# The residual as the first term of the experts' sums, and a final norm that reads PSUM

## What is computed

```
x = x + mixed @ w_merge_out
h = rms_norm(x, norm2_g)
logits = h @ router_w + router_b            # 32 experts, the top 4 of each token
f = sum over the top 4 of gate * (act @ w_down[e] + b_down[e])
    act = (up + 1) * (g * sigmoid(1.702 * g)),  [g, up] = h @ w_gate_up[e] + b_gate_up[e], clamped at 7
x = x + f
y = rms_norm(x, final_norm_g)
```

## Time and profile before

| | |
|---|---|
| median of 3 runs | 1508.98 us (1508.48 to 1509.87) |
| the profiled execution | 1509.2 us, its span 1507.0 us |
| mean granted clock of TensorE | 0.95 |
| PE busy | 1401.1 us, 93% |
| PEld busy | 655.4 us, 43% |
| DVE busy | 353.7 us, 23% |
| ACT busy | 178.6 us, 12% |
| HBM read | 440.53 MB |

### The profile page before, as it was taken

One profiled execution on the slowest core, in us unless ns is written; L12 is line 12 of the kernel. 1 busy time (PEld: TensorE's weight loads), 2 busy tenths in 40 slices (PEclk: granted clock), 3 DMA queues, 4 the chain that ended last, 5 costly groups with the idle time before them and its releaser, 6 DMA issues.

```text
span 1507.0 us, 15701 instructions
## 1 busy us (share of the span) xinstructions
PE 1401.1 (93%) x6182; PEld 655.4 (43%) x6183; DVE 353.7 (23%) x935; ACT 178.6 (12%) x348; POOL 36.6 (2%) x44
## 2 busy tenths in 40 slices
PE   6997998998989999999998999999999999999886
PEld 4775776896444333333332333333333333332222
DVE  2496626333551101111010101100110011001002
ACT  2011252210010100001000001000001000000002
POOL 3101001000000000000000000000000000000000
PEclk9999997987966999999999999999999999999998
DMA  9648212014455999999980999999999999999925
GB/s 251 139 139 88 84 56 57 1 57 141 170 217 204 416 416 418 417 417 414 418 358 2 414 415 416 418 416 416 416 418 417 415 415 417 418 415 415 414 105 214
DMA packets 86364, 446.52 MB, mean 296 GB/s; under 512 B 9456, under 2 KB 10368, under 8 KB 53360
## 3 DMA queue, kind: packets, MB, share of 16 engines
q1 hardware_dynamic: 82960, 436.45, 73.8%
q0 software_dynamic: 2720, 7.13, 1.9%
q10 hardware_dynamic: 576, 1.37, 0.3%
HBM read 440.53 MB, written 4.39 MB: 295 GB/s over the span
## 4 chain that ended last, share of the span: by engine, by line
PE 72%; DMA 21%; DVE 3%; issue 2%; SPq 1%; ACT 1%; ACTq 0%; DVEq 0%
PE ps L1048 21%; DMA arena<-in_w_gate_up 17%; PE ps L1076 10%; PE ps L711 10%; PE ps L1027 6%; PE ps L1086 3%; PE ps L929 2%; PE ps L1041 2%; DMA arena<-in_w_down 1%; DMA arena<-in_w_main 1%; SPq L359 1%; PE ps L922 1%; PE ps L816 1%; PE ps L750 1%; PE ps L1127 1%
## 5 line engine op out<-in xcount | busy, mean ns | idle before, releaser
L1048 PE MATMUL ps<-arena 128*64 128x512 f32 x2048 | 460.0, 602 | 13.1 <-DMA arena<-in_w_gate_up 12.9
L1048 PEld LDWEIGHTS ps<-arena 128*64 128x64 f32 x2048 | 145.6, 138 | 326.2 <-issue 277.9
L1076 PE MATMUL ps<-arena 128*64 128x512 f32 x1024 | 227.3, 595 | 10.1 <-issue 6.8
L1590 DVE TENSOR_SCALAR arena<-ps 128x512 f32<-128x512 f32 x32 | 22.1, 692 | 726.4 <-PE ps L1048 726.4
L711 PE MATMUL ps<-arena 128*128 128x320 f32 x576 | 161.8, 444 | 14.2 <-DMA arena<-in_w_main 8.5
L1076 PEld LDWEIGHTS ps<-arena 128*64 128x64 f32 x1024 | 82.8, 137 | 132.4 <-issue 127.1
L711 PEld LDWEIGHTS ps<-arena 128*128 128x128 f32 x576 | 112.4, 196 | 63.3 <-issue 19.3
L1027 PE MATMUL ps<-arena 128*128 128x256 f32 (+1 forms) x384 | 121.7, 447 | 0.0
L1027 PEld LDWEIGHTS ps<-arena 128*128 128x128 f32 (+1 forms) x384 | 67.8, 204 | 66.3 <-issue 61.9
L1086 PE MATMUL ps<-arena 128*128 128x512 f32 (+1 forms) x192 | 79.4, 617 | 1.3 <-ACT arena L619 1.3
L608 ACT ACTIVATE arena<-ps 128x512 f32<-128x512 f32 x32 | 19.1, 597 | 478.7 <-PE ps L1048 478.7
(11 more groups left out here) (288 smaller groups left out, 920.1 us busy)
## 6 DMA issues: line engine op xcount, KB each, us to landing
arena<-in_w_gate_up SPq DMA_DIRECT2D x256, 1024.0 KB, 20.2
arena<-in_w_down SPq DMA_DIRECT2D x128, 1024.0 KB, 23.8
arena<-in_w_main SPq DMA_DIRECT2D x40, 512.0 KB, 3.6
arena<-in_w_merge_out SPq DMA_DIRECT2D x1, 3072.0 KB, 10.5
arena<-in_w_conv_out POOLq DMA_DIRECT2D x1, 2048.0 KB, 13.1
arena<-in_w_delta_out SPq DMA_DIRECT2D x1, 2048.0 KB, 9.0
out_delta_s<-arena POOLq DMA_DIRECT2D x1, 2048.0 KB, 15.1
arena<-in_xT SPq DMA_DIRECT2D x1, 1280.0 KB, 6.6
```

The costliest lines, as they stand in the source:

```text
L1048: m = pe.matmul(ps[SLOTS * (q % 2):SLOTS * (q % 2 + 1), q // 2, :], tokens[:, k], w[:, q * 512:(q + 1) * 512], start=False, stop=(k == KD ...
L1076: m = pe.matmul(ps[SLOTS * c:SLOTS * (c + 1), 2, :], actT[:, r, a * SLOTS:(a + 1) * SLOTS], pieces[UPS + r][:, a, c * 512:(c + 1) * 512], ...
L1590: ts(upb, ps[:, 1, :], 1.0 + LIMIT, 1.0 - LIMIT, ALU.min, ALU.max).then_inc(chain, 1)
```

## The change

`bias` gets a matmul with the identity ahead of the one with the gates: `xs` of the tile is the moving operand, so the residual is the first term of the sum in the bank, and the biases are added to it. `add_sums` is gone. ScalarE squares the sums where they stand in PSUM as soon as the tile's last `combine` is through; for `t` 2, whose halves lie on different partitions, in two instructions with a second row sum (`stat_2`), which VectorE adds. `final_norm` scales from PSUM too. A new semaphore `rest_over` tells ScalarE that the code of `any_rest` is behind VectorE.

```
@@ -156,7 +156,7 @@
         con_at = at[0]
         ident = take(P)
         iota = take(PLACED)
-        stat, stat_y, stat_t = take(NT), take(NT), take(NT)
+        stat, stat_2, stat_y, stat_t = take(NT), take(1), take(NT), take(NT)
         late_at = at[0]
         h2 = take(2, D)
         actb = take(512)
@@ -189,6 +189,9 @@
         late_y, late_xt = upb[0:2 * LATE], sil[0:2 * LATE]
         late_actT = actT[:, :, 0:2 * LATE]
         assert moe[0] <= base
+        def sums(t):
+            return ps[:, 3 + 2 * t:5 + 2 * t, :].rearrange("p b n -> p (b n)")
+
         def rows(t):
 
 
@@ -671,9 +674,15 @@
 
             for t in range(NT):
                 n = TILES[t][1]
-                act.wait_ge(sem("added"), 2 * (t + 1))
-                act.activation(yout[0:n, t], xs[0:n, t], ACT.Square,
-                               accum_out=stat[0:n, t:t + 1]).then_inc(sem("x2_ss"), 1)
+                act.wait_ge(sem("rest_over"), 1)
+                act.wait_ge(sem("c_mm"), 2 * NT * (E // 2 - 1) + 2 * (t + 1))
+                if t < 2:
+                    act.activation(yout[0:n, t], sums(t), ACT.Square,
+                                   accum_out=stat[0:n, t:t + 1]).then_inc(sem("x2_ss"), 1)
+                else:
+                    act.activation(yout[0:n, t, 0:512], ps[0:NS, 7, :], ACT.Square, accum_out=stat[0:n, t:t + 1])
+                    act.activation(yout[0:n, t, 512:D], ps[NS:P, 7, :], ACT.Square,
+                                   accum_out=stat_2[0:n]).then_inc(sem("x2_ss"), 1)
                 root(stat_y[0:n, t:t + 1], stat[0:n, t:t + 1], 8 + t)
 
         @block.tensor
@@ -991,8 +1000,11 @@
                 return pe.transpose(ps[0:E, 0, tok(t)], gates[rows(t), t, 0:E], ident[rows(t), rows(t)])
 
             def bias(t, c, out):
+                n = TILES[t][1]
+                pe.matmul(out, ident[0:n, 0:n], xs[0:n, t, c * 512:(c + 1) * 512],
+                          start=True, stop=False, skip_group_check=True)
                 pe.matmul(out, gmT[0:E, tok(t)], bdn[0:E, c * 512:(c + 1) * 512],
-                          start=True, stop=True, skip_group_check=True).then_inc(sem("bd_mm"), 1)
+                          start=False, stop=True, skip_group_check=True).then_inc(sem("bd_mm"), 1)
 
             pe.wait_ge(sem("x2_done"), 6)
             pe.wait_ge(sem("gates_ready"), 2)
@@ -1628,6 +1640,7 @@
                     over(late_later[0:1].unsqueeze(1), 1, E, LATER), ALU.is_gt))
             link(dve.tensor_reduce(hot_most[0:1], ps[0:1, 1, NT * E:(NT + 1) * E], mybir.AxisListType.X, ALU.max))
             link(ts(hot_now[0:1], hot_most[0:1], float(REST), None, ALU.is_gt))
+            step.done(dve.memset(stat_2, 0.0))
             dve.memset(stat, 0.0).then_inc(sem("routed"), 1)
             ts(bg[2 * E:], bg[2 * E:], 1.0, None, ALU.add).then_inc(sem("bg_ready"), 1)
             for u in range(4):
@@ -1681,26 +1694,26 @@
             def final_norm(t):
                 n, col = TILES[t][1], slice(t, t + 1)
                 dve.wait_ge(sem("x2_ss"), NT + t + 1)
+                if t == 2:
+                    link(tt(stat[0:n, col], stat[0:n, col], stat_2[0:n], ALU.add))
                 ts(stat[0:n, col], stat[0:n, col], 1.0 / D, EPS, ALU.mult, ALU.add).then_inc(sem("root_in"), 1)
                 root(stat_y[0:n, col], stat[0:n, col], stat_t[0:n, col], 8 + t)
-                stt(out=yout[0:n, t], in0=xs[0:n, t], scalar=stat_y[0:n, col], in1=fg[0:n],
-                    op0=ALU.mult, op1=ALU.mult).then_inc(sem("y_out"), 1)
-
-            def add_sums(t):
-                n = TILES[t][1]
-                dve.wait_ge(sem("c_mm"), 2 * NT * (E // 2 - 1) + 2 * (t + 1))
-                for c in range(2):
-                    part = xs[0:n, t, c * 512:(c + 1) * 512]
-                    src = ps[:, SUM_BANKS[t][c], :] if t < 2 else ps[NS * c:NS * (c + 1), SUM_BANKS[t][c], :]
-                    tt(part, part, src, ALU.add).then_inc(sem("added"), 1)
-
-            add_sums(0)
-            add_sums(1)
+                if t < 2:
+                    stt(out=yout[0:n, t], in0=sums(t), scalar=stat_y[0:n, col], in1=fg,
+                        op0=ALU.mult, op1=ALU.mult).then_inc(sem("y_out"), 1)
+                else:
+                    for c in range(2):
+                        i = stt(out=yout[0:n, t, c * 512:(c + 1) * 512], in0=ps[NS * c:NS * (c + 1), 7, :],
+                                scalar=stat_y[0:n, col], in1=fg[0:n, c * 512:(c + 1) * 512],
+                                op0=ALU.mult, op1=ALU.mult)
+                        if c == 0:
+                            step.done(i)
+                    i.then_inc(sem("y_out"), 1)
+
+            dve.sem_inc(sem("rest_over"), 1)
             dve.wait_ge(sem("ld_fg"), 16)
-            final_norm(0)
-            add_sums(2)
-            final_norm(1)
-            final_norm(2)
+            for t in range(NT):
+                final_norm(t)
 
 
 INS = [("xT", (P, KD, N)), ("x_prompt", (NP, D)), ("x_sample", (NS, D)),
```

## The result

The changed kernel takes 1525.24 us (median of 4 runs, 1517.56 to 1528.66); the kernel before, run beside it, 1508.73 us (4 runs, 1505.98 to 1509.87). The ratio is 1.0104, with an interval of 1.0068 to 1.0139: 15.7 us slower, 10.3 to 21.0. The forecast was 1521.0, with a range of 1516.0 to 1523.5. The direction and the two large terms came out; the median lies above the range. In a later set (`after_again`) the same kernel has its median of 6 runs at 1521.18 us, inside the range, with the same ratio. The profiled execution took 1523.56 us, its span is 1521.4 us.

What follows compares the result with a forecast made beforehand. TensorE, at its low clock in front of the experts, was taken to hold back the weight stream. 1509.2 + 14.6 (front) - 2.3 (tail) = 1521.5, less 0.2 for the median and 0.3 for a shorter low clock: 1521.0 us, range 1516.0 to 1523.5.

Steps and rivals of the forecast that it cites:

- the two large terms: The sum's two main terms: 14.6 us added in front of the experts, 2.3 us given back in the tail.
- The bound: In front of the experts TensorE, at its low clock, sets when the weight stream starts; added work delays every later transfer equally.
- The rival that the time is absorbed: Slack at the stream's start hides the added front time, leaving only the tail's gain: 1506.7 us; chance 0.03.
- The identity matmuls and their changes: Prompt tiles in `bias`: four new matmuls, 6.83 us, plus seven changes of matmul height at 0.295, 2.07 us.
- The samples' four slots: Samples' matmuls in `bias` (`t` 2): alternating shapes do not overlap, four slots of 1.90 us, 5.69 us more.
- The rival with 10.8: Samples' matmuls in `bias` overlap after all: front adds 10.8 us instead of 14.6, 1517.5 us; chance 0.25.
- The tail: After the last combine: adds go, squares and scalings read PSUM, last scaling ends at 1501.35, not 1503.67; 2.3 us gained.
- The experts' term: Among the experts: all work stays, nothing in the sum; clock dips in the two late blocks give 1 to 2 us of range.
- The own range of the main case: Main case of 1521.0 us, without sample overlap or early clock rise: 1519.5 to 1523.5 us, chance 0.60.
- The early rise: Identity matmuls raise TensorE's clock within `bias`, before the gathers (L1027): 1501 us, or 1507 if only at its end; chance 0.08.
- Tail without gain: The change does not shorten the tail: 14.6 us alone, 1523.6 us; chance 0.04, shared with more changeover cost than summed.

Runs made afterwards that it cites:

- gates_twice: The kernel before with each gates' matmul of `bias` issued twice, no identity, so twelve matmuls of one height; 1519.39 us, ratio 1.0067.
- after_aligned: The changed kernel with `stat_2` taken behind all other buffers, so that these lie as in the kernel before; 1519.64 us, ratio 1.0076.
- ids_last: The changed kernel with all gates' matmuls of `bias` first, then the six identity matmuls in one run; 1499.52 us, ratio 0.9956.
- ids_first: The changed kernel with all identity matmuls of `bias` first, then all gates' matmuls; 1513.05 us, ratio 1.0037.
- before_delay: The kernel before with one unused full-height matmul ahead of the first gather; 1497.18 us, ratio 0.9942.
- after_delay: The changed kernel with one unused full-height matmul ahead of the first gather; 1526.15 us, ratio 1.0121.
- warm_up: The kernel before with four unused matmuls of 128 rows and 512 columns ahead of the first gather; 1495.85 and 1497.64 us, ratios 0.9923 and 0.9946.

## Why the prediction was right or wrong

**The bound: right.** TensorE in front of the experts held the stream: its 14.57 us more moved the first expert by as much, and SyncE's longest wait for it was 27.3 us after 27.9. The rival that the time is absorbed is out.

**The identity matmuls and their changes: right.** 4 x 1.707 and 7 x 0.295 were the periods in the trace, 2.00 us a matmul in place of 1.71.

**The samples' four slots: right,** 1.90 us each, and `gates_twice` shows what the other choice would have been: with equal heights they overlap, two slots. TensorEngine Tiling (Array Packing), Key Properties, in the Trainium skill, which says that a change of tiling mode drains TensorE, agrees with both; it has no price, and the runs give it: 0.295 us at the low clock in the prompt's tiles, and 3.97 us for the lost overlap of the samples. The rival with 10.8 is out.

**The tail: right in mechanism, 0.24 us too hopeful.** The scaling of tile 0 came 5.65 us behind the start of the combine, where it was 6.83: 1.18 earlier, not 1.28. The period to tile 1 was 2.39 (2.36 forecast), to tile 2 2.54 (2.56), and its two halves took 1.53, not 1.3 to 1.4. A scaling of 1024 from PSUM took 1.28 us, what it took from SBUF. VectorE: DVE Perf Modes, in the Trainium skill's section on the TRN2 errata, would have it longer from PSUM; no row here shows that. ScalarE's square was 1.02 us from PSUM for 1.04 to 1.06 from SBUF.

**The experts' term: this is the step that failed.** The working said that all expert work stays and gave the dips of the clock in the late blocks 1 to 2 us of range. The instructions did stay; their time did not. Their time was 1012.09 and 1011.69 us in the two traces of before and 1013.58 to 1016.15 in the three of after and the one of `after_aligned`: 1.5 to 4.5 more, 3.4 from mean to mean. Put into the sum, 14.57 + 3.4 - 2.06 = 15.9 us, against 15.7 measured. The working counted falls of the clock in the late blocks alone. A spell outside one leaves the stream its 414 GB/s where it occurs and is paid in the next late block, where SyncE waits for TensorE: 2.6 us of the 3.5 between the two first traces. Why after has the later spell stays open. The own range of the main case, 1519.5 to 1523.5, was also narrower than a median of four executions of a kernel whose executions span some 10 us: that of `after_again` lies in it, so that the first one fell outside is in part chance.

**The early rise: false for this kernel, right as a mechanism.** In after the clock stayed at 0.50 over 23.6 us of `bias` and 25.3 us of gathers with TensorE busy throughout. The arguments against it (half of the stretch is the 32-row matmul, with changes between) stand: `ids_last`, the same matmuls unmixed, had the rise within them and came out 6.6 us under before, where 8 had been worked out for a rise within `bias` and 2 for one at its end. The point from which it decides was named as the start of L1027; `ids_first` confirms it from the other side, as it had the clock at 1.00 until 445.0, where the gathers started, and lost it there: 5.6 us over before by its ratio, where `ids_last` is 6.6 under. TensorE: Matmul & The Clock Gate, of the Trainium skill, has in its Part 1 a throttled default that activity releases, and says that the point of the release varies from run to run. The runs agree with the second (two of twelve of `before_delay` went without the gain, by their times). The first it does not bear out for this stretch: TensorE was busy 23.59 of 23.59 us in `bias` without a rise.

**Tail without gain:** out by the trace (2.06), not settled by the times.

## What to carry to other kernels

Before one folds an add into a matmul, one should ask what order the new matmul stands in: the same six cost 14.6 us between matmuls of another height and paid for themselves behind them, directly ahead of the next high matmuls. Where TensorE goes into its critical stretch at the low clock, one to four full-height matmuls with no other use, put directly ahead of it, are the cheapest experiment of all: here 0.5 to 0.8% from two lines. And where a stream of transfers pauses at some block until TensorE is through, and TensorE is as busy ahead of it as here (300.6 of 307.6 us), a delay of TensorE ahead of that block is paid at the block, even if the stream shows no gap where the delay occurs.

## What the hardware showed that was not expected

- With one matmul of 1.87 us (128 rows, 512 columns) behind 9.0 us of 32-row matmuls the granted clock went from 0.50 to 1.00 2.4 us after its end, in the trace of `before_delay`, and 9.7 us were gained; in that of `after_delay` it did not. Without it the gathers, also of 128 rows, with 256 columns and their changes, did not bring it in 25 us.
- The rise can be lost as fast: in `ids_first` the clock was 1.00 during 4.6 us of 32-row matmuls and 0.50 from their end on, with TensorE never idle.
- One kernel has executions 6.6 us apart at a point where nothing differs but waits and the granted clock.
- The fastest kernels leave the change out: `warm_up` (1495.85 and 1497.64 us) and `before_delay` (1497.18) against 1507 to 1509 before and 1521 to 1525 after. Not tried were the combination of the tail of after with such a matmul, and the identities in TensorE's idle time ahead of `turn_gates`.
